# Rotary rows packed and spread by transfers within SBUF in place of an exchange matrix on TensorE

## The reference

```python
def partial_rope(x, pos):
    half = ROPE_DIM // 2                      # 8
    inv = jnp.power(ROPE_THETA, -jnp.arange(half, dtype=jnp.float32) * 2.0 / ROPE_DIM)
    ang = pos.astype(jnp.float32)[:, None] * inv[None, :]
    cos = jnp.cos(ang)[None, :, None, :]
    sin = jnp.sin(ang)[None, :, None, :]
    x1, x2, rest = xf[..., :half], xf[..., half:ROPE_DIM], xf[..., ROPE_DIM:]
    out = jnp.concatenate([x1 * cos - x2 * sin, x2 * cos + x1 * sin, rest], axis=-1)
...
    dq = partial_rope(rms_norm(heads(dq, DSA_HEADS), dsa_q_norm), pos)
    dk = partial_rope(rms_norm(dk, dsa_k_norm)[:, :, None], pos)[:, :, 0]
    iq = partial_rope(heads(iq, IDX_HEADS), pos)
    ik = partial_rope(ik[:, :, None], pos)[:, :, 0]
    o_a = dsa_attention(dq, dk, dv, iq, iw, ik, k_top)
```

## Time and profile before

| | us |
|---|---|
| median of 3 runs | 1365.91 (1364.96 to 1367.18) |
| the profiled execution | 1366.64 |
| its span in the profile | 1364.8 |
| PE busy | 1341.2 (98% of the span) |
| PE weight load busy (beside PE) | 1214.8 (89%) |
| DVE busy | 643.6 (47%) |
| ACT busy | 507.9 (37%) |
| POOL busy | 533.7 (39%) |

### The profile page before, as it was taken

The page is one execution under the profiler, slowest core; times in us unless marked ns, Lnnn a source line. Parts: engine busy times, 40 slices in busy tenths (PEclk is TensorE's granted clock), DMA queues, the critical chain, the costliest instruction groups (busy, mean ns, idle before and its releaser), DMA issues.

```text
span 1364.8 us, 22941 instructions
## 1 busy us (share of the span) xinstructions
PE 1341.2 (98%) x8702; PEld 1214.8 (89%) x8702; DVE 643.6 (47%) x1076; ACT 507.9 (37%) x817; POOL 533.7 (39%) x260
## 2 busy tenths in 40 slices
PE   7999999999999999999999999999999999999998
PEld 7989999899999999999998988987878888888887
DVE  5688668654333333322223699984643333332000
ACT  4444447633222222322224545365432222232212
POOL 3543301134444444444437441201444444444444
PEclk9999999999999999999999999999999999999999
DMA  5222200122222222233222111100222222332324
GB/s 185 63 63 78 72 23 32 32 78 78 93 92 92 91 81 88 92 97 104 92 92 91 65 62 47 47 32 31 93 93 92 92 92 94 98 100 94 107 93 154
DMA packets 32169, 112.46 MB, mean 82 GB/s; under 512 B 3696, under 2 KB 4080, under 8 KB 31984
## 3 DMA queue, kind: packets, MB, share of 16 engines
q1 hardware_dynamic: 31392, 110.59, 24.9%
q10 hardware_dynamic: 720, 1.09, 0.2%
HBM read 109.57 MB, written 2.10 MB: 82 GB/s over the span
## 4 chain that ended last, share of the span: by engine, by line
PE 54%; issue 31%; POOL 8%; DVE 5%; ACT 1%; POOLq 0%; DMA 0%; SPq 0%; DVEq 0%; ACTq 0%
PE ps L900 19%; PE ps L906 10%; POOL wlo L783 8%; PE ps L990 5%; PE ps L991 5%; PE ps L996 5%; PE ps L1085 2%; PE ps L1004 1%; PE ps L1111 1%; PE ps L1064 1%; DVE feat L1630 1%; PE ps L1094 1%; PE ps L1014 1%; PE ps L956 1%; PE ps L1149 1%
## 5 line engine op out<-in xcount | busy, mean ns | idle before, releaser
L783 POOL TENSOR_TENSOR wlo<-raw,whi 128x1024 fp32r<-128x1024 f32 x202 | 500.2, 2477 | 824.6 <-ACT whi L1279 824.1
L1279 ACT ACTIVATE whi<-raw 128x1024 fp32r<-128x1024 f32 x202 | 213.8, 1059 | 583.2 <-PE ps L906 544.2
L900 PE MATMUL ps<-xhi,whi 128*128 128x264 f32 (+1 forms) x1096 | 327.9, 322 | 7.0 <-ACT whi L1279 6.9
L900 PE MATMUL ps<-xlo,whi 128*128 128x264 f32 (+1 forms) x1096 | 326.5, 322 | 0.0
L900 PEld LDWEIGHTS ps<-xhi,whi 128*128 128x128 f32 x1096 | 206.8, 189 | 24.3 <-ACT whi L1279 6.7
L900 PEld LDWEIGHTS ps<-xlo,whi 128*128 128x128 f32 x1096 | 206.7, 189 | 16.1
L906 PE MATMUL ps<-xhi,wlo 128*128 128x264 f32 (+1 forms) x1096 | 195.4, 321 | 0.4 <-POOL wlo L783 0.2
L990 PE MATMUL ps<-xhi,whi 128*128 128x264 f32 (+1 forms) x632 | 182.5, 317 | 0.3 <-DVE feat L1581 0.3
L906 PEld LDWEIGHTS ps<-xhi,wlo 128*128 128x128 f32 x1096 | 162.9, 188 | 17.3 <-issue 1.0
L991 PE MATMUL ps<-xlo,whi 128*128 128x264 f32 (+1 forms) x632 | 172.4, 301 | 0.0
L900 PE MATMUL ps<-hlo,whi 128*128 128x264 f32 (+1 forms) x528 | 157.5, 321 | 0.0
(11 more groups left out here) (180 smaller groups left out, 1695.3 us busy)
## 6 DMA issues: line engine op xcount, KB each, us to landing
raw<-in_weights SPq DMA_DIRECT2D x202, 512.0 KB, 3.5
out_hT<-h SPq DMA_DIRECT2D x8, 256.0 KB, 4.2
h<-in_hT SPq DMA_DIRECT2D x4, 264.0 KB, 6.2
h<-in_hT ACTq DMA_DIRECT2D x4, 264.0 KB, 5.8
cst<-in_consts SPq DMA_DIRECT2D x1, 1046.0 KB, 9.8
par_all<-in_params SPq DMA_DIRECT2D x1, 144.0 KB, 9.4
par_all<-in_params SPq DMA_DIRECT2D x1, 140.0 KB, 9.6
cst<-in_consts SPq DMA_DIRECT2D x1, 128.0 KB, 4.9
```

Source lines behind the costliest of these rows:

```text
L783: nc.gpsimd.tensor_tensor(wlo[:, b], raw[:, b], whi[:, b].bitcast(F32), ALU.subtract).then_inc(split_done, 1)
L900: nc.tensor.matmul(bank(bank_no, cut.stop - cut.start), whi[:, b, k % KT], x(k)[t][:, cut], start=(first and k == ks[0] and t == 0), stop= ...
L1279: return nc.scalar.activation(whi[:, b], raw[:, b], ACT.Copy).then_inc(hi_done, 1)
```

## The change

**TensorE.** The exchange matrix and the step `rope` on TensorE are gone: five jobs of two float32 matmuls for each layer.

**Layout.** Within each pair of heads of the tiles `DKIK`, `IQ` and `DQ`, the first head's 16 rotated features are moved to its end (`turned_last` on the weights, the same for the norm's gains), so the rotated rows of both heads lie together in partitions 48 to 79 (`ROPE_ROWS`).

**Transfers.** SP copies, for each of the five tiles, those 32 rows to `xnb[:, 0]` and, in four transfers of 8 rows with the halves exchanged, to `xnb[:, 1]` (`gather`). Three tiles are packed side by side in 96 partitions, then two in 64. DVE runs three operations for each group (`rope(n)`), with all operands in SBUF. SP puts the results back: six transfers for the first group (four to `kk`, two to `feat`), two for the second (`spread`). `copies` are now four transfers of 48 rows from `feat` to `kk`, issued by SP, and may run before the rotation. That makes 37 transfers within SBUF for each layer, in the queue that also loads the weights.

**Waits.** `index(1, 0)`, `logits(0, ...)`, `fox_log` and the first two `silu` wait for `spread` instead of `roped`. SP waits in its list for `normed`, `feat_ready` and `roped`.

**Order.** `plan` has new steps and costs and new `BIAS` weights, so every engine's list is laid anew. The rest of the small edits is: the scan in `fox_log` no longer reads a row of ones, and the constants are 128 columns shorter.

```diff
-ROPE_ORDER = (DKIK, IQ, IQ + 1, DQ, DQ + 1)
-
-INDEX_ROPES = 3
+
+
+
+ROPED = ((DKIK, IQ, IQ + 1), (DQ, DQ + 1))
+ROPE_ORDER = ROPED[0] + ROPED[1]
+ROPE_ROWS = slice(48, 80)
...
-            with sp.Fori(1, STREAM // 2) as j:
-                for b in range(2):
-                    load_unit(j * 2 + b, b)
+            for b in range(2):
+                load_unit(2 + b, b)
+            for l in range(DEPTH):
+                ev = layer[l]
+
+                def proj(k, hf, p):
+                    load_unit(l * UNITS + k + 4, k % 2)
+
+                def group_rows(k):
+                    n = 0 if k in ROPED[0] else 1
+                    at = 32 * ROPED[n].index(k)
+                    return n, at
+
+                def gather(k):
+
+                    n, at = group_rows(k)
+                    if k in NORMS:
+                        sp.wait_ge(ev.normed, NORMS[k] + 1)
+                    sp.wait_ge(ev.feat_ready, 2 * k + 2)
+                    if n:
+                        sp.wait_ge(ev.spread[0], 16 * 6)
+                    src = feat[ROPE_ROWS, place(k)]
+                    sp.dma_start(xnb[at:at + 32, 0], src).then_inc(ev.packed[n], 16)
+                    for q in range(4):
+                        row = ROPE_ROWS.start + 8 * (q ^ 1)
+                        sp.dma_start(xnb[at + 8 * q:at + 8 * q + 8, 1], feat[row:row + 8, place(k)]).then_inc(ev.packed[n], 16)
+
+                def spread(n):
+
+                    sp.wait_ge(ev.roped, n + 1)
+                    if n == 0:
+                        for tile, rows, at in ((0, slice(48, 64), 0), (1, slice(64, 80), 0), (3, slice(64, 80), 16), (2, slice(48, 64), 16)):
+                            sp.dma_start(kk[rows, tile], xnb[at:at + 16, 0]).then_inc(ev.spread[n], 16)
+                    for k in ROPED[n]:
+                        if k != DKIK:
+                            at = group_rows(k)[1]
+                            sp.dma_start(feat[ROPE_ROWS, place(k)], xnb[at:at + 32, 0]).then_inc(ev.spread[n], 16)
+
+                def copies():
+
+                    sp.wait_ge(ev.normed, NORMS[DKIK] + 1)
+                    sp.wait_ge(ev.feat_ready, 2 * DKIK + 2)
+                    low, high = slice(0, 48), slice(80, 128)
+                    for tile, rows, of in ((0, low, low), (1, high, low), (3, high, high), (2, low, high)):
+                        sp.dma_start(kk[rows, tile], feat[of, place(DKIK)]).then_inc(ev.copied, 16)
+
+                do = dict(proj=proj, gather=gather, spread=spread, copies=copies)
+                for step in ORDER[l][DMAE]:
+                    do[step[0]](*step[1:])
+                first = l * UNITS + N_PROJ + 4
+                last = (l + 1) * UNITS + 4 if l < DEPTH - 1 else STREAM
+                with sp.Fori(0, (last - first) // 2) as j:
+                    for b in range(2):
+                        load_unit(j * 2 + (first + b), b)
...
-                def rope(k):
-                    b0, done = job_begin(("rope", k))
-                    if k in NORMS:
-                        pe.wait_ge(ev.normed, NORMS[k] + 1)
-                    pe.wait_ge(ev.feat_ready, 2 * k + 2)
-                    for hf in range(2):
-                        ins = nc.tensor.matmul(bank(b0 + hf, HALF), cols(C_ROT, 128),
-                                               feat[:, place(k), hf * HALF:(hf + 1) * HALF], start=True, stop=True)
-                    ins.then_inc(done, 1)
...
                     if (i, hd) == (1, 0):
-                        pe.wait_ge(ev.roped, INDEX_ROPES)
-                        pe.wait_ge(ev.copied, 2)
+                        pe.wait_ge(ev.spread[0], 16 * 6)
+                        pe.wait_ge(ev.copied, 16 * 4)
                         pe.wait_ge(ev.zeroed, CLEARED["clear_keys"])
...
-                            pe.wait_ge(ev.roped, len(ROPES))
-                            pe.wait_ge(ev.copied, 2)
+                            pe.wait_ge(ev.spread[0], 16 * 6)
+                            pe.wait_ge(ev.spread[1], 16 * 2)
+                            pe.wait_ge(ev.copied, 16 * 4)
...
-                def copies():
-                    act.wait_ge(ev.roped, ROPES[DKIK] + 1)
-                    nc.scalar.activation(kk[64:128, 1], kk[0:64, 0], ACT.Copy).then_inc(ev.copied, 1)
-                    nc.scalar.activation(kk[0:64, 2], kk[64:128, 3], ACT.Copy).then_inc(ev.copied, 1)
-
...
-                def rope(k):
-                    b0, taken, n = wait_done(("rope", k))
-                    dve.wait_ge(ev.feat_ready, 2 * k + 2)
-                    chain(nc.vector.tensor_tensor(xnb[:, 0], feat[:, place(k)], cols(C_COS, N), ALU.mult))
-                    nc.vector.tensor_tensor(halves(xnb[:, 1]), two_banks(b0), halves(cols(C_SIN, N)), ALU.mult).then_inc(taken, 1)
-                    dve.wait_ge(taken, n)
-                    if k == DKIK:
-                        chain(nc.vector.tensor_tensor(kk[0:64, 0], xnb[0:64, 0], xnb[0:64, 1], ALU.add))
-                        nc.vector.tensor_tensor(kk[64:128, 3], xnb[64:128, 0], xnb[64:128, 1], ALU.add).then_inc(ev.roped, 1)
-                    else:
-                        nc.vector.tensor_tensor(feat[:, place(k)], xnb[:, 0], xnb[:, 1], ALU.add).then_inc(ev.roped, 1)
-                    dve.wait_ge(ev.roped, ROPES[k] + 1)
+                def rope(n):
+                    dve.wait_ge(ev.packed[n], 16 * 5 * len(ROPED[n]))
+                    rows = slice(0, 32 * len(ROPED[n]))
+                    x, other = xnb[rows, 0], xnb[rows, 1]
+                    chain(nc.vector.tensor_tensor(x, x, cols(C_COS, N, rows), ALU.mult))
+                    chain(nc.vector.tensor_tensor(other, other, cols(C_SIN, N, rows), ALU.mult))
+                    nc.vector.tensor_tensor(x, x, other, ALU.add).then_inc(ev.roped, 1)
...
+def turned_last(w):
+
+    heads = w.reshape(w.shape[0], -1, 64)
+    return np.concatenate([np.roll(heads[:, i], -16 if i % 2 == 0 else 0, axis=1) for i in range(heads.shape[1])], axis=1)
+
+
...
-    c[:, C_COS:C_COS + N] = 1
-    for base in (0, 64):
-        for j in range(half):
-            lo, hi = base + j, base + half + j
-            c[hi, C_ROT + lo] = -1
-            c[lo, C_ROT + hi] = 1
-            for r in (lo, hi):
-                c[r, C_COS:C_COS + N] = np.cos(ang[j])
-                c[r, C_SIN:C_SIN + N] = np.sin(ang[j])
+    for r in range(128):
+        c[r, C_COS:C_COS + N] = np.cos(ang[r % half])
+        c[r, C_SIN:C_SIN + N] = np.sin(ang[r % half]) * (1 if r // half % 2 else -1)
```

More of the change, by code:

```diff
@@ L148, in chains_of_steps @@
         "norm": [("norm", k) for k in NORM_ORDER],
-        "rope": [("rope", k) for k in ROPE_ORDER],
+        "gather": [("gather", k) for k in ROPE_ORDER],
+        "rope": [("rope", n) for n in range(2)],
+        "spread": [("spread", n) for n in range(2)],
         "copies": [("copies",)],
@@ L186, in work @@
         keys = keys_to(a[1])
-    ropes = [(("rope", k), DVEE) for k in ROPE_ORDER]
+    spreads = [(("spread", n), DMAE) for n in range(2)]
     def evicted(k):
@@ L225, in work @@
                 (DVEE, dve_us(N, True) * (2 if k in (FQ, FQ + 1, FK, FK + 1) else 1), [] if k >= GV else [evicted(k)])]
+    if kind == "gather":
+        k = a[0]
+        return [(DMAE, 0.8, [(("norm", k), DVEE) if k in NORMED else evicted(k)] + ([(("spread", 0), DMAE)] if k in ROPED[1] else []))]
     if kind == "rope":
-        k = a[0]
-        return [(PE, 0.9, [(("norm", k), DVEE) if k in NORMED else evicted(k)]), (DVEE, 2 * dve_us(N, True) + dve_us(N), [])]
+        return [(DVEE, 3 * dve_us(N, True), [(("gather", k), DMAE) for k in ROPED[a[0]]])]
+    if kind == "spread":
+        return [(DMAE, 0.4 if a[0] else 1.0, [(("rope", a[0]), DVEE)])]
     if kind == "copies":
-        return [(ACTE, 2 * act_us(N), [(("rope", DKIK), DVEE)])]
+        return [(DMAE, 0.7, [(("norm", DKIK), DVEE)])]
     if kind == "turn_tile":
@@ L245, in work @@
     if kind == "fox_log":
-        return [(ACTE, 2.8, [(("turn_tile", SMALL), PE), evicted(SMALL)] + ropes), (DVEE, 2.0, [])]
+        return [(ACTE, 2.8, [(("turn_tile", SMALL), PE), evicted(SMALL)] + spreads), (DVEE, 2.0, [])]
     if kind == "clear_keys":
@@ L265, in work @@
         used = [(("index", (n - 2) // 4 + 1, (n - 2) % 4), DVEE)] if n >= 2 else []
-        return [(PE, sum(pe_fp32(c) for c in cut), ropes[:INDEX_ROPES] + [(("copies",), ACTE), (("clear_keys",), POOLE)]),
+        return [(PE, sum(pe_fp32(c) for c in cut), spreads[:1] + [(("copies",), DMAE), (("clear_keys",), POOLE)]),
                 (ACTE, act_us(keys, True), used),
@@ L342, in work @@
     raise ValueError(kind)
-AUX_KINDS = ("prenorm", "norm", "rope", "turn_tile", "gate", "index", "logits", "turn", "meta_turn", "turn_k", "gla_att", "gla_out",
+AUX_KINDS = ("prenorm", "norm", "turn_tile", "gate", "index", "logits", "turn", "meta_turn", "turn_k", "gla_att", "gla_out",
              "gla_kv", "back")
-WIDE_KINDS = ("prenorm", "norm", "rope", "turn_tile", "gate", "turn_k", "gla_att", "gla_out")
```

(9 more changed lines are left out.)

27 lines of the change are left out of this document (13 added, 14 removed).

## The result

The changed kernel takes **1370.08 us** (median of 7 runs, 1368.06 to 1371.77), the kernel before 1365.91 (7 runs, 1364.91 to 1367.18): a ratio of 1.0030, 95% interval 1.0018 to 1.0041. It is slower by 0.3%, where 1358.5 was forecast, with 1353.0 to 1363.2 as the range. The profiled execution took 1368.06, the least of the seven.

A forecast was written before the change was run, and what follows sets the result against it. TensorE was taken as the bound, busy 1341.2 of 1364.8 us. Terms -9.0 - 2.2 - 1.7 + 1.4 + 2.4 + 1.7 = -7.4 us took 1365.91 to 1358.5, range 1353.0 to 1363.2.

The forecast's parts named there:

- all on the path: TensorE's ten exchange jobs, about 0.9 us each: removing them was to shorten the run by the full 9.0 us.
- gone in all: On TensorE: 9.0 us of exchange jobs, 2.2 of wait and 1.7 of lost clock removed, together 12.9 us.
- about 0.36 with the gap; 0.5 at the program's start: SP's queue: us to issue one transfer, taken from weight loads since the trace had no transfer within SBUF.
- The landing: Time from a short SBUF transfer's issue to its arrival, taken as 1.7 us, with ends of 1.3 and 3.4.
- The lock at `rope(0)`: DVE operations with two SBUF inputs and POOL's splits exclude each other; second-layer wait 2.3 to 2.7 us, 0.4 without it.
- the second rival: Transfers in both layers land in 3.4 us instead of 1.7, the clock falls twice: 1362.7 us, chance 0.13.
- the first's: The rival with no lock at `rope(0)`, or transfers quick enough to slip ahead of it: 1353.4 us, chance 0.22.
- Later choices of the planner: Half-microsecond waits moving about in the new order: counted as zero, with 2 us either way in the range.
- the old wait: TensorE's wait for DVE's norm at unit 5's exchange job in the kernel before, 2.2 us, expected to go.
- The clock: Half clock on TensorE after a long wait: 1.7 us charged once, for the second layer's wait.
- the first wait: TensorE at `index(1, 0)` in the first layer, waiting for the first group's transfers: 1.1 to 1.8 us, taken as 1.4.
- Rival 3: SP's queue serves transfers one after another: slower beyond t near 0.9 us, near 1400 at t = 1.7; chance 0.06.

The follow-up runs named there:

- gather3: The changed kernel with rotated pairs in neighbouring rows, exchanged copy in 2 transfers instead of 4, 27 transfers a layer instead of 37: 1364.14 us, ratio 0.9985.
- after_index_later: The changed kernel with the first layer's first two index jobs moved behind unit 5's first half on TensorE and unit 4's rounding on ScalarE: 1364.60 us, ratio 0.9990.
- after_scalar_spread: The changed kernel with two of the first spread's six transfers in the first layer issued by ScalarE instead of SyncE: 1369.10 us, ratio 1.0016.
- before_no_rotation: The kernel before without exchange matmuls, their waits on TensorE, or VectorE's rotations of four of the five tiles: 1359.90 us, ratio 0.9943.
- before_no_exchange: The kernel before in its own order, its ten exchange jobs without their matmuls, TensorE's waits kept, rotation not computed: 1364.38 us, ratio 0.9984.
- before_no_exchange_no_wait: The kernel before without the exchange matmuls and also without TensorE's waits at those ten places: 1362.08 us, ratio 0.9970.
- after_both_later: The changed kernel with the first layer's first index jobs moved later and the second layer's first rotations behind unit 3's eviction: 1359.58 us, ratio 0.9950.

## Why the prediction was wrong

- **A job at "about 0.9 us", ten of them at 9.0 us, "all on the path".** PE's busy time fell by 9.2. "All on the path" failed in the order of before: 2.1 us, or 4.4 with the waits gone. In the new order about 8 us came out without packing and spreading, where the prediction's "gone in all" was 12.9. So most of this term held in the kernel that it was made for, but with DVE's lighter load, which I counted as zero and which the run without rotations shows to be worth 2 to 3 in the old order.
- **Issue at "about 0.36 with the gap; 0.5 at the program's start".** This is the first of the two steps that failed. Loads and transfers within SBUF were put on one scale: it is 0.61 and, with 8 rows, up to 0.69. The landing, taken as 1.7, was 2.0, so the transfers overlap and only their issues are in series. In the first layer the last gather transfer started near 40.8 instead of 37.4 to 37.95, and the wait was 5.0 (3.8 without the one slow issue) instead of 1.4; in the second 3.5 instead of 2.4. With the half clock behind them the prediction had 1.4 + 2.4 + 1.7 = 5.5 us for what the transfers cost; the kernel without packing and spreading is 12.2 below the changed one.
- **The lock at `rope(0)`** did not decide. The packing landed so late that the split was already over (three times 0.71 in the second layer); in the first it had ended at 40.71, and the third operation took 1.02 beside a copy on POOL that runs from 43.90. The lock is there: the second group's first operation, 64 partitions, took 1.82 in place of 0.71 beside a split, and in gather3, where the packing is early enough, `rope(0)` itself meets it in both layers (1.23 and 2.90). (Where the prediction says that without the lock the sum would be the second rival's, it means the first's, 1353.4.)

```profile
756.71 1.82 DVE L1662 TENSOR_TENSOR xnb<-xnb,cst 64x532 f32<-64x532 f32 x1 [2.85 <-DMA xnb<-feat]
...
755.57 2.40 POOL L844 TENSOR_TENSOR wlo<-raw,whi 128x1024 fp32r<-128x1024 f32 x1 [4.09 <-ACT whi L1331]
```

- **"Later choices of the planner move some half-microsecond waits about; I count that as zero, with 2 us either way in the range."** This is the second step that failed. They came to 4.4: idle grew by 10.7, of which the two stops less the old wait are 5.0 + 3.5 - 2.2 = 6.3. `turn_k` alone waits 4.2 more (4.8 for 0.6). The kernel without packing and spreading has the same waits, and its 1357.92 is 4.9 above the 1353.0 that the 12.9 gone would give. With 6.7 from the transfers' cost this makes up the 11.6 between 1358.5 and 1370.08. Why `turn_k` is late in the new order stays open.
- **The clock**: charged once, 1.7. In the profiled execution it fell once, but behind the first stop. In after_index_later and after_scalar_spread it fell behind the second stop, at 2.5 us and more. Some of the other six runs of the changed kernel, 0.6 to 3.7 longer than the profiled one, likely had that as well: four of them have a mean clock of 0.995 or 0.996 against its 0.997. No trace of them shows the place.
- **The sum**, against the profiled execution: forecast -7.4, measured 1368.06 - 1366.64 = +1.4. Of the 8.8 between, 3.6 is the first wait, 1.1 the second and 4.4 the small waits (9.1 together, with 0.2 to 0.3 the other way in PE's own work and in rounding). The median adds 2.0 to that.
- **Rival 3** had the place and the form, a fixed time for each transfer in SP's queue, with 2.1 us for every 0.1 of issue; I gave it 0.06 and put its threshold at a t near 0.9. By its own rule 0.61 to 0.69 costs only some 2 to 7 us; with the half clock and the small waits on top, it was enough. Its 1400 was far off. That a gain of 7.4 stood on waits worked out to tenths, with an issue cost that no row showed, called for a wider range than 1353.0 to 1363.2.

## What to carry to other kernels

Swapping a short job on a full engine for a chain of transfers buys time only if whoever needs the result is placed as far behind as the chain is long, at the cost of one issue per transfer, in series: measure that issue first, put it in the planner's table, and lay the order by it. Cut the number of transfers rather than their bytes. And before counting removed work as gain, look stage by stage at which other engine is full: where one is, nothing comes out until that one is relieved too.

## What was not expected of the hardware

- An SBUF to SBUF transfer holds the issuing queue for 0.51 to 0.61 us (0.66 to 0.69 with 8 partitions), about twice a load of 512 KB in an idle queue (0.33), and for 33 KB the same as for 66 KB. ScalarE's queue took 1.45 for two. The landings still overlap, 2.0 us from the issue for most.
- A transfer whose partitions are every second row costs no more: 1.22 us for two, as for two of 32 rows in a block.

```profile
32.68 0.59 SPq L800 DMA_DIRECT2D xnb<-feat  x1
33.31 1.22 SPq L803 DMA_DIRECT2D xnb<-feat  x2
```

- The length of a stop does not say whether the half clock follows. It came during or within 1.2 us behind stops of 1.8 (before_no_rotation), 1.9, 2.1, 2.2, 2.3, 2.4, 3.5, 3.7, 3.8 and 5.0 us. It did not come behind stops of 1.9 (before_no_exchange, at 36.2) and 2.3 (before_no_exchange_no_wait, at 73.7), nor behind that of 3.5 in the second layer of the changed kernel, where the same stop in after_index_later had it. So stops of one length can differ by 2.5 us in what they cost. It also came where no stop of 0.6 us or more stood within 90 us ahead, at 139.6 in after_index_later, and cost 1.6 us; after_both_later, with the same order in that layer, had full clock there. What decides stays open.
